# Output projection of the mixing stage as three fp32r products, with new places and load times for its rows

## The chip, the cores and the metric

One core of a Trainium2 chip. The metric is the device time of one execution of the whole layer, in microseconds (us), median of several runs. The core has five engines that run their own instruction streams and wait for each other on semaphores: TensorE (matrix products and transposes, in the profile PE, its weight loads PEld), VectorE (DVE), ScalarE (ACT), GpSimd (POOL) and SyncE (SP), which issues nearly all transfers. PSUM has eight banks of 512 float32 columns, called ps[:, 0] to ps[:, 7].

## What is computed

A hybrid layer on 1024 tokens of width 1024, with 16 meta tokens ahead:

```python
h = concat(meta, x)
u = rmsnorm(h, norm_mix)
z = u @ w_in
y_a = rwkv7_mix(z[..., :P_A], ...)       # 8 heads of 64, a recurrence over the tokens
y_b = retention_mix(z[..., P_A:], ...)   # 4 heads of 128, a recurrence over chunks
mixed = concat(y_a, y_b)
h = h + mixed @ w_out                    # (1024 x 1024) @ (1024 x 1024): the changed product
u = rmsnorm(h, norm_ffn)
h = h + hier_moe(u, ...)                 # top-1 group, top-2 of 32 experts, gated MLP
out = rmsnorm(h, norm_final)[:, 16:]
```

All inputs and outputs are float32.

## The kernel before

Three stages follow each other with a barrier of all engines between them. There are no planners: the order on each engine is the order in which its function issues its instructions.

**project** (lines 224 to 1226). u = rmsnorm(h) is made in nine tiles t: 16 meta rows, then eight tiles of 128 rows. For a tile, SP loads x into h_in[t % 3] (load_x, L323, which waits for u_ready), ScalarE squares and sums it (square, L454), VectorE adds epsilon and later multiplies by the root and the gain (norm, L721), GpSimd takes the power -0.5 (L699), TensorE turns it into PSUM (turn, L1064), ScalarE copies the high part u_hi (high, L463) and VectorE subtracts it for the low part u_lo (low_rows, L732). w_in comes in 30 blocks of 128 columns, split in w_hi (ScalarE, split, L471) and w_lo (VectorE, low, L739). A unit (n, r) (unit, L1073) is block n times one of three ranges of tokens, in 24 products (w_hi u_hi, w_hi u_lo, w_lo u_hi for 8 slices) of 344 or 352 columns. The order of the first units and turns is written out at L1191 to L1213. One load brings all the constants (L350), the identity that the transposes need among them, and TensorE begins by waiting for it.

**mix** (lines 1254 to 2261). Eight tiles t = 1 to 8 of 128 tokens, each with the recurrences of both head groups. On every engine a function body(t) holds one tile's work; inside it stands the closing work of the tile before, n = t - 1: normalising y and the gate, the output projection, the residual, the second rmsnorm and the routing. TensorE's body(t) is, in order: cross products (g_ab, g_ak, g_rk), ret_rows_0(n), chunks for l2, l2_t and q_m, l4, l4_t, l3_t, turn_y(n), chunks l8 and inv4, rwkv_rows_0(n), ret_rows_1(n), chunk inv8, rwkv_rows_1(n), turn_ret(t), the chunks x_t, x_m, z0, x2_t, ret_scores(t+1), x3_t, ret_keys(t+1), turn_h2(n), w, ranks and route(n), ret_inner(t+1), to_features (m_t, rz, n_m), ret_cross(t+1), the states and y. "Chunks" are 16 products of 64x64x64. ret_rows and rwkv_rows are the four calls of project(n, c, ...) at L1999 to L2005: each multiplies four transposed 128x128 blocks of mixed rows (mixed_b from the retention, mixed_a from the rwkv part) with 512 columns of w_out, in float32:

```python
mm = pe.matmul(ps[:, 6 + c, :], rows[:, k_, :], w_out[:, at_, c * 512:(c + 1) * 512], ...)
```

The mixed rows come to SBUF by one ScalarE copy each from the bank where they were turned (mixed_rows_a, mixed_rows_b, L1458 to L1462). On VectorE the chain inv_1, inv_2, inv_3, inv_4, inv_ready (L1772 to L1801) builds a triangular inverse step by step from what TensorE's chunks give, with keep, b_centre, choose_group, residual(n, 0), b_gate, choose_first, choose_second and residual(n, 1) between its steps.

The rows of a tile are 24 feature rows (a, b, k, r, q, kr, four each; fm) and 9 token rows (v, a, bh, kh, kd, rv, rg, gate, bonus; tm). Both have two places, by t % 2, and SP loads them a tile ahead: load_fm and load_tm (L1345 to L1353), in the loop at L1398. w_out is one load of 4 MB (L1377). 15 blocks of zeros are stored to y_slots from h_t at the start (L1386). At the end SP loads the first expert's gate and up matrices in four pieces each (first_weights, L1391), the one after y0_done(7), the other after inv_ready(8). They go to the place of tm1 and what stands behind it.

**dispatch_and_experts** (from L2264). Gathers each expert's rows, and makes three fp32r products with high and low parts (product, L2807) for every expert. It begins when the routing's last result, slot_row, and the stores of u2 are there.

## Time and profile before

| | us |
|---|---|
| three timed runs | 1551.6, 1559.14, 1559.41 (median 1559.14) |
| the profiled execution | 1555.97, its span 1554.1 |
| TensorE busy, share of the span | 92% |
| VectorE, ScalarE, GpSimd busy | 1023.9, 698.9, 563.2 |
| mean granted TensorE clock | 0.957 |
| stages in the span | project to 459, mix 464 to 919, experts from 921 |

All times below are of the profiled execution, in us from the span's start. A row of the timeline has the start, the time from the first start to the last end of what is merged in the row, the engine, the line and the operation with what it writes and reads, and in brackets the idle time of the engine ahead of it and what ended that. TensorE's products overlap by their fill, so the distance between two starts is the price of one in a stream, not its own duration.

### The profile page before, as it was taken

To read this page: it belongs to the slowest core of one execution; us is meant where nothing else is said; L and a number is where in the kernel's file an instruction comes from. 1 tells how busy PE (TensorE), PEld (TensorE's weight loads), DVE (VectorE), ACT (ScalarE), POOL (GpSimd) and SP (SyncE) were. 2 spreads that over 40 slices of the span, in tenths; PEclk is the share of its full clock that TensorE was granted. 3 is DMA by queue.
4 is the path that set the end of the run, shared out by engine and by line. 5 is a ranking of instruction groups with operands and counts; after the bars stand their busy time and mean duration, and the time that the engine had idled before them with its cause. 6 is when DMAs were issued, how large, how long until landed. Compare 5 with 4: busy or idle time off the path is not lost. (4 is left out here: it accounts for less than half of the span.)

```text
span 1554.1 us, 32619 instructions
## 1 busy us (share of the span) xinstructions
PE 1426.6 (92%) x14222; PEld 1225.4 (79%) x14222; DVE 1023.9 (66%) x1174; ACT 698.9 (45%) x678; POOL 563.2 (36%) x198
## 2 busy tenths in 40 slices
PE   5999999999989899998999858999999999999990
PEld 4899999999988777687778637788888888888870
DVE  5456555444213656666577536999989899777757
ACT  4434442212212112121222126777777777777752
POOL 1001101000000000000000027777787878999975
PEclk9999999999997999999999869999999999999995
DMA  5124354543429732333232329999999999999968
GB/s 206 42 96 140 120 157 131 158 127 111 130 63 343 253 106 96 105 130 132 69 115 72 111 90 423 413 405 408 411 412 402 407 400 406 416 413 420 413 249 326
DMA packets 113575, 366.24 MB, mean 236 GB/s; under 512 B 10896, under 2 KB 70672, under 8 KB 100384
## 3 DMA queue, kind: packets, MB, share of 16 engines
q1 hardware_dynamic: 100640, 318.33, 54.2%
q0 software_dynamic: 6912, 25.17, 4.6%
q10 hardware_dynamic: 5904, 20.97, 3.3%
q8 instruction: 96, 1.57, 0.4%
q14 instruction: 23, 0.19, 0.0%
HBM read 295.47 MB, written 68.98 MB: 235 GB/s over the span
## 5 line engine op out<-in xcount | busy, mean ns | idle before, releaser
L1085 PE MATMUL ps<-u_hi,w_hi 128*128 128x352 f32 (+1 forms) x720 | 239.4, 332 | 6.9 <-DVE u_lo L736 6.8
L1085 PE MATMUL ps<-u_lo,w_hi 128*128 128x352 f32 (+1 forms) x720 | 235.0, 326 | 0.0
L1085 PE MATMUL ps<-u_hi,w_lo 128*128 128x352 f32 (+1 forms) x720 | 234.0, 325 | 0.0
L2426 POOL TENSOR_TENSOR down_lo<-down_raw,down_hi 128x1024 fp32r<-128x1024 f32 x31 | 151.2, 4878 | 62.2 <-ACT down_hi L2495 62.2
L2426 POOL TENSOR_TENSOR gate_lo<-gate_raw,gate_hi 128x1024 fp32r<-128x1024 f32 x32 | 161.4, 5045 | 22.1 <-ACT gate_hi L2495 22.1
L2593 DVE TENSOR_TENSOR down_lo<-down_raw,down_hi 128x3072 fp32r<-128x3072 f32 x31 | 125.5, 4049 | 41.8 <-ACT down_hi L2495 41.8
L1085 PEld LDWEIGHTS ps<-u_hi,w_hi 128*128 128x128 f32 x720 | 138.6, 193 | 13.9 <-issue 10.6
L2593 DVE TENSOR_TENSOR gate_lo<-gate_raw,gate_hi 128x3072 fp32r<-128x3072 f32 x32 | 130.8, 4086 | 13.7 <-ACT gate_hi L2495 13.4
L1085 PEld LDWEIGHTS ps<-u_lo,w_hi 128*128 128x128 f32 x720 | 138.6, 192 | 0.0
L1085 PEld LDWEIGHTS ps<-u_hi,w_lo 128*128 128x128 f32 x720 | 138.5, 192 | 0.0
L2593 DVE TENSOR_TENSOR up_lo<-up_raw,up_hi 128x3072 fp32r<-128x3072 f32 x32 | 126.0, 3937 | 15.1 <-ACT up_hi L2495 14.7
L1438 POOL TENSOR_TENSOR mix_stat<-mix_stat,minus_half 128x4 f32<-128x4 f32 x8 | 8.2, 1024 | 344.6 <-DVE mix_stat L1715 344.6
L2495 ACT ACTIVATE gate_hi<-gate_raw 128x4096 fp32r<-128x4096 f32 x32 | 116.4, 3638 | 17.1 <-SPq L2354 13.9
L2495 ACT ACTIVATE down_hi<-down_raw 128x4096 fp32r<-128x4096 f32 x31 | 112.7, 3636 | 19.6 <-ACT y_out L2516 19.6
L2426 POOL TENSOR_TENSOR up_lo<-up_raw,up_hi 128x1024 fp32r<-128x1024 f32 x32 | 116.6, 3644 | 4.0 <-ACT up_hi L2495 3.5
L2495 ACT ACTIVATE up_hi<-up_raw 128x4096 fp32r<-128x4096 f32 x32 | 116.1, 3627 | 0.3 <-DMA up_raw<-in_moe_w_up 0.3
L2811 PE MATMUL ps<-gate_hi,x_hi 128*128 128x512 f32 x256 | 102.2, 399 | 6.9 <-POOL gate_lo L2426 6.7
L2811 PE MATMUL ps<-up_hi,x_hi 128*128 128x512 f32 x256 | 102.9, 402 | 3.3 <-DVE up_lo L2593 2.3
L2811 PE MATMUL ps<-gate_lo,x_hi 128*128 128x512 f32 x256 | 100.8, 394 | 0.0
L2811 PE MATMUL ps<-gate_hi,x_lo 128*128 128x512 f32 x256 | 100.8, 394 | 0.0
L2811 PE MATMUL ps<-up_hi,x_lo 128*128 128x512 f32 x256 | 100.2, 391 | 0.0
L2811 PE MATMUL ps<-up_lo,x_hi 128*128 128x512 f32 x256 | 99.7, 390 | 0.0
(397 smaller groups left out, 3041.7 us busy)
## 6 DMA issues: line engine op xcount, KB each, us to landing
down_raw<-in_moe_w_down SPq DMA_DIRECT2D x32, 2048.0 KB, 11.0
gate_raw<-in_moe_w_gate SPq DMA_DIRECT2D x31, 2048.0 KB, 10.5
up_raw<-in_moe_w_up SPq DMA_DIRECT2D x31, 2048.0 KB, 9.6
tm_rows<-tm_stage SPq DMA_DIRECT2D x32, 512.0 KB, 3.3
y_slots<-y_out ACTq DMA_DIRECT2D x31, 512.0 KB, 11.6
w_raw<-in_w_in SPq DMA_DIRECT2D x30, 512.0 KB, 3.7
tm<-tm_rows SPq DMA_DIRECT2D x8, 1792.0 KB, 9.2
y_slots<-h_t SPq DMA_DIRECT2D x15, 512.0 KB, 7.8
```

Of the source, the lines that this page charges most:

```text
L1085: mm = pe.matmul(z_of(n, r_), w[n % 3][:, k_, :], a[:, k_, c0:c1], start=(k_ == 0 and i == 0), stop=(k_ == KD - 1 and i == 2))
L1438: pool.tensor_tensor(stat[:, 5, 0:HB], stat[:, 4, 0:HB], half[:, 0:HB], ALU.pow).then_inc(sem("rstd_b"), 1)
L2426: pool.tensor_tensor(lo[e % 2][:, cut:, :], raw[e % 2][:, cut:, :], hi[:, cut:, :].bitcast(F32), ALU.subtract).then_inc(sem(f"{name}_lo2_r ...
L2495: act.activation(hi[:], raw[b][:], ACT.Copy).then_inc(sem(f"{name}_hi_ready"), 1)
L2593: dve.tensor_tensor(lo[b][:, :cut, :], raw[b][:, :cut, :], hi[:, :cut, :].bitcast(F32), ALU.subtract).then_inc(sem(f"{name}_lo_ready"), 1)
L2811: mm = pe.matmul(ps[:, bank, :], a[:, k, :], w[:, k, cols], start=(k == 0 and i == 0), stop=(k == ks - 1 and i == 2))
```

## The change

In the projection of the mixing stage w_out is kept in a high part w_hi and a low part w_lo (both fp32r), and so are the mixed rows (a_hi, a_lo, b_hi, b_lo). Each float32 product becomes three fp32r products. ScalarE makes the high parts, VectorE the low parts of the rows and four of w_out's eight slices, GpSimd the other four:

```diff
+                def project(c, hi, lo, at_, first, last):
+                    cols = slice(c * 512, (c + 1) * 512)
+                    for k_ in range(4):
+                        for i, (rows, w) in enumerate(((hi, w_hi), (lo, w_hi), (hi, w_lo))):
+                            mm = pe.matmul(ps[:, 6 + c, :], rows[:, k_, :], w[:, at_ + k_, cols],
+                                           start=(first and k_ == 0 and i == 0), stop=(last and k_ == 3 and i == 2))
...
                 def rwkv_rows_0(n):
-                    pe.wait_ge(sem("mixed_a_t"), n)
-                    project(n, 0, mixed_a, range(4), False, True).then_inc(sem("proj0_done"), 1)
+                    if n == 1:
+                        pe.wait_ge(sem("w_out_lo_ready_a"), 4)
+                    pe.wait_ge(sem("a_hi_ready"), n)
+                    pe.wait_ge(sem("a_lo_ready"), n)
+                    project(0, a_hi, a_lo, 0, False, True).then_inc(sem("proj0_done"), 1)
```

VectorE (in body(t); low_a also behind a_gate in the tail, where choose_first follows it):

```diff
+                def low_a(n):
+                    dve.wait_ge(sem("a_hi_ready"), n)
+                    tt(a_lo[:].rearrange("p k t -> p (k t)"), ps[:, 7, :], a_hi[:].rearrange("p k t -> p (k t)").bitcast(F32), ALU.subtract, "a_lo_ready")
...
                     tt(inv[:], inv[:], ps[:, 4, :], ALU.add, "inv_3")
+                    if n:
+                        low_a(n)
                     keep(t, 0)
...
                     dve.tensor_copy(x_m[:], ps[:, 4, :]).then_inc(sem("x_m_ready"), 1)
                     if n:
+                        low_b(t, 5)
                         h_variance(n)
                         norm(n)
...
                     tt(x_p[:], x_p[:], ps[:, 5, :], ALU.add, "x_p_ready")
+                    if t == 1:
+                        low_b(1, 7)
...
                        bank_pair(2), ALU.add, "rz_t_ready")
+                    if t == 1:
+                        for k in range(4, 8):
+                            w_low(k)
                     state_first(t)
```

ScalarE's w_high(k) (1024 elements each) stand in body(1): k = 0, 1 ahead of mixed_rows_b(1), 2, 3 behind it, 4 to 7 behind m_t. GpSimd has w_lo of k = 0 to 3 behind rstd_b(1).

The rows get one place each, except v and r, which have two by the parity of t. Each load waits for the last use of the tile before:

```diff
+                def load_next(t):
+                    sp.wait_ge(sem("g_rk_done"), t - 1)
+                    if t >= 3:
+                        sp.wait_ge(sem("rz_t_ready"), t - 2)
+                        sp.wait_ge(sem("y0_done"), t - 2)
+                    load_fm(t, "a", "k")
+                    load_fm(t, "r", "r")
+                    load_tm(t, "v", "v")
...
+                for t in range(1, NT):
                     n = t - 1
+                    if n:
+                        if t + 1 < NT:
+                            load_next(t + 1)
+                        sp.wait_ge(sem("mixed_a_ready"), n)
                         load_tm(t, "gate", "bonus")
                     if t + 1 < NT:
+                        sp.wait_ge(sem("mixed_b_ready"), t)
+                        load_tm(t + 1, "rg", "rg")
+                        sp.wait_ge(sem("z0_a_done"), t)
+                        load_tm(t + 1, "a", "a")
+                    if n:
+                        store_h2(n)
+                        load_h(t)
+                        store_u2(n)
+                    if t + 2 < NT:
+                        load_retention(t + 2)
+                    sp.wait_ge(sem("n_m_done"), t)
+                    if t + 1 < NT:
+                        load_tm(t + 1, "bh", "kh")
+                    if t + 2 < NT:
+                        load_heads(t + 2)
+                    for i in range(2 * n, min(2 * t, EXTRA)):
+                        sp.dma_start(y_dram[(NE + i) * P:(NE + i + 1) * P, :].rearrange("p (a c) -> p a c", c=2 * P),
+                                     zero[:].unsqueeze(1).to_broadcast([P, D // (2 * P), 2 * P])).then_inc(sem("zero_stored"), 16)
+                sp.wait_ge(sem("mixed_b_ready"), NTX)
+                first_weights(0, "moe_w_gate")
+                first_weights(1, "moe_w_up")
                 store_h2(NTX)
                 store_u2(NTX)
```

load_retention(t) loads kd behind kv_done(t-1) and rv behind inner_done(t-1), load_heads(t) loads q and kr behind cross_done(t-1). The blocks of zeros are written two per tile from a row of 256 zeros. Several temporaries share a place: q_m that of ak_t, x_m that of ld_t, x_t that of ld, x2_t that of l4_t, x_p that of lo, rz_t that of l2, w_m that of z0. The meta rows' semaphores of tile 1 are merged into three counters.

In **project**, every x tile has a place of its own (in rows that are used later) and its statistics a column of their own, u has four places, load_x waits for nothing, and the epsilon is added by ScalarE behind the square:

```diff
                 def load_x(t):
-                    if t >= 3:
-                        sp.wait_ge(sem("u_ready"), t - 2)
-                    sp.dma_start(h_in[t % 3], x[(t - 1) * P:t * P, :]).then_inc(sem(f"h_loaded{t % 3}"), 16)
+                    sp.dma_start(h_in[t], x[(t - 1) * P:t * P, :]).then_inc(sem(f"h_loaded{t}"), 16)
...
-                sp.dma_start(consts[:], d["consts"]).then_inc(sem("consts_loaded"), 16)
+                sp.dma_start(ident, d["consts"][:, 0:P]).then_inc(sem("ident_loaded"), 16)
+                load_x(2)
                 load_w(0)
-                load_x(2)
+                load_x(3)
                 load_w(1)
...
+                load_w(2)
+                sp.dma_start(consts[:, P:], d["consts"][:, P:]).then_inc(sem("consts_loaded"), 16)
...
+                    act.wait_ge(sem("mean_square"), t + 1)
+                    act.activation(stat[0:w, 1, t:t + 1], stat[0:w, 0, t:t + 1], ACT.Copy, bias=1e-6).then_inc(sem("mean_eps"), 1)
```

On ScalarE the order becomes square 0, 1, 2, high 0, square 3, high 1, split 0, high 2, square 4, high 3, split 1. On VectorE: norm 1, low_rows 0, norm 2, norm 3, low_rows 1, low_rows 2, low 0, low_rows 3, low 1. On TensorE weights(1) moves from ahead of unit(0, 0) to ahead of unit(1, 0), and the wait for the other constants stands ahead of block 2.

## Rows read from the trace of the kernel before

**Rows 1.** The page's first part: busy us, share of the span, instructions.
```profile
PE 1426.6 (92%) x14222; PEld 1225.4 (79%) x14222; DVE 1023.9 (66%) x1174; ACT 698.9 (45%) x678; POOL 563.2 (36%) x198
```

**Rows 2.** Windows: length, busy us (x) of PE, PEld, DVE, ACT, POOL, clock, DMA.
```profile
467.00:479.00 12.00, 10.86 (x242) 10.27 (x236) 4.80 (x14) 2.03 (x6) 0.00 (x0) 0.50 1.00 332
...
527.00:576.00 49.00, 47.54 (x1056) 37.49 (x1054) 28.16 (x49) 11.08 (x19) 3.20 (x3) 1.00 0.36 115
...
1000.00:1450.00 450.00, 447.54 (x2113) 369.50 (x2112) 405.00 (x214) 346.16 (x176) 377.18 (x101) 1.00 1.00 409
```

**Rows 3.** The line L1438, once per mixing tile: ns min/median/max, first and last start.
```profile
L1438 POOL TENSOR_TENSOR mix_stat<-mix_stat,minus_half x8: 1007/1007/1143, 506.4 to 850.1; 128x4 f32<-128x4 f32 x8
```

**Rows 4.** Timeline, two weight loads in the projection: start, us, engine, line, operation.
```profile
788.30 0.19 PEld L2003 LDWEIGHTS ps<-w_out,mixed_b 128*128 128x128 f32 x1 [0.24 <-issue]
...
788.73 0.19 PEld L2003 LDWEIGHTS ps<-w_out,mixed_b 128*128 128x128 f32 x1 [0.24 <-issue]
```

**Rows 5.** Timeline of TensorE, expert stage: the first and last of 22 products.
```profile
1199.77 0.39 PE L2811 MATMUL ps<-down_hi,hid_lo 128*128 128x512 f32 x1
...
1204.54 0.39 PE L2811 MATMUL ps<-down_hi,hid_lo 128*128 128x512 f32 x1
```

**Rows 6.** Timeline, the middle of a steady tile.
```profile
748.94 0.60 ACT L1456 ACTIVATE mixed_a<-ps 128x512 f32<-128x512 f32 x1 [0.92 <-PE ps L1885]
...
749.03 0.42 DVE L1535 TENSOR_TENSOR kept<-state,decay 128x256 f32<-128x256 f32 x1
...
750.84 3.70 PE L2003 MATMUL ps<-w_out,mixed_a 128*128 128x512 f32 x8
...
753.63 0.19 DVE L1644 TENSOR_TENSOR t_log<-logits,t_pick 128x32 f32<-128x32 f32 x1
...
755.28 0.68 DVE L1535 TENSOR_TENSOR inv<-inv,ps 128x512 f32<-128x512 f32 x1
...
757.91 1.15 PE L1895 MATMUL ps<-inv,l 64*64 64x64 f32 x32
```

**Rows 7.** Timeline, the tail of the mixing stage.
```profile
889.86 0.60 ACT L1456 ACTIVATE mixed_a<-ps 128x512 f32<-128x512 f32 x1 [9.93 <-PE ps L1885]
...
904.17 0.69 DVE L1535 TENSOR_TENSOR h<-h_res,ps 128x512 f32<-128x512 f32 x1 [3.40 <-PE ps L2003]
...
918.77 0.18 DVE L1876 CAST slot_row<-slot_sum 128x32 int32<-128x32 f32 x1
```

**Rows 8.** Timeline, the start of the kernel.
```profile
11.05 1.06 ACT L460 ACTIVATE tm_stage<-tm_stage 128x1024 f32<-128x1024 f32 x1 [1.17 <-DMA tm_stage<-in_x]
...
24.40 0.63 PE L1085 MATMUL ps<-u_hi,w_hi 128*128 128x352 f32 x1 [3.70 <-DVE u_lo L736]
...
40.78 0.62 PE L1085 MATMUL ps<-u_hi,w_hi 128*128 128x344 f32 x1 [3.11 <-DVE u_lo L736]
```

**Rows 9.** Timeline of VectorE, the first mixing tile.
```profile
513.60 0.69 DVE L1535 TENSOR_TENSOR memory<-scratch,ps 128x512 f32<-128x512 f32 x1
...
515.84 1.22 DVE L1535 TENSOR_TENSOR w_m<-z,ps 128x1024 f32<-128x1024 f32 x1 [1.55 <-PE ps L1895]
...
525.09 0.42 DVE L1535 TENSOR_TENSOR state<-kept,ps 128x256 f32<-128x256 f32 x1 [5.98 <-PE ps L1929]
```

**Rows 10.** The page's costliest groups: count, busy us, mean ns of one, idle before.
```profile
L2593 DVE TENSOR_TENSOR down_lo<-down_raw,down_hi 128x3072 fp32r<-128x3072 f32 x31 | 125.5, 4049 | 41.8 <-ACT down_hi L2495 41.8
...
L2426 POOL TENSOR_TENSOR up_lo<-up_raw,up_hi 128x1024 fp32r<-128x1024 f32 x32 | 116.6, 3644 | 4.0 <-ACT up_hi L2495 3.5
```

**Rows 11.** Transfers issued from 459 to 530: count, size, median us to landing.
```profile
fm<-fm_rows SPq DMA_DIRECT2D x2, 512.0 KB, 8.6
```

**Rows 12.** Timeline, SP's last loads of the stage and TensorE's last n_m product.
```profile
865.92 13.98 SPq L1395 DMA_DIRECT2D up_raw<-in_moe_w_up x4
...
875.96 0.45 PE L1920 MATMUL ps<-tm 64*64 64x64 f32 x8
```

**Rows 13.** Timeline of TensorE, a gap inside a steady tile.
```profile
737.00 0.47 PE L1907 MATMUL ps<-fm 64*64 64x64 f32 x2 [3.99 <-issue]
```

More of the change, by code:

```diff
@@ L234, in project @@
         tm = tile(s, "tm_stage", [P, 6, SEQ])
-        h_in, u, gain = [tm[:, b, :] for b in range(3)], [tm[:, 3 + b, :] for b in range(2)], tm[:, 5, :]
+        u, gain = [tm[:, 1 + b, :] for b in range(4)], tm[:, 5, :]
         by_tile = lambda i: tm[:, i, :].rearrange("p (t c) -> p t c", c=P)
@@ L1195, in _ @@
                 weights(0)
-                weights(1)
                 pe.wait_ge(sem("u_hi_ready"), 4)
@@ L1201, in _ @@
                 turn(5)
+                weights(1)
                 unit(1, 0)
@@ L1278, in mix @@
+        v_even, gate_bonus, r_even = sb("v_even", DA), sb("gate_bonus", 2, DA), sb("r_even", 4, P)
+        zero = sb("zero", 2 * P)
+        w_hi = tile(s, "w_out_hi", [P, KD, D], F32R)
+        w_lo, w_raw = env["two_names"](s, "w_out_lo", [P, KD, D], F32R, "w_out_raw", [P, KD, D])
+        assert nc.sbuf_base <= first_at
+        router_w = sb("router_w", KD, NR)
         gain, router_b, ffn_gain = sb("norm_ffn_rows", D), sb("router_b", NR), sb("ffn_gain", KD)
         h_in, h2, u2, h2_t = sb("h_res", D), sb("h2", D), sb("u2", D), sb("h2_t", KD, P)
-        mixed_a, mixed_b = sb("mixed_a", 4, P), [sb(f"mixed_b{b}", 4, P) for b in range(2)]
@@ L1281, in mix @@
-        ld_t, ld, lo, ak_t, rb_t, rk_t, l2, l4_t, inv, x_m, x_t, x2_t, x_p, q_m, rz_t, y = (
-            sb(n, DA) for n in ("ld_t", "ld", "lo", "ak_t", "rb_t", "rk_t", "l2", "l4_t", "inv",
-                                "x_m", "x_t", "x2_t", "x_p", "q_m", "rz_t", "y"))
-        l8, scratch = l2, sb("scratch", DA)
+        a_hi, a_lo, b_hi, b_lo = (sb(n, 4, P, dt=F32R) for n in ("a_hi", "a_lo", "b_hi", "b_lo"))
+        ld_t, ld, lo, rb_t, rk_t, l2, inv, y = (sb(n, DA) for n in ("ld_t", "ld", "lo", "rb_t", "rk_t", "l2", "inv", "y"))
@@ L1286, in mix @@
+        l8, rz_t, q_m, x_m, x_t, x2_t, x_p, scratch = l2, l2, ak_t, ld_t, ld, l4_t, lo, sb("scratch", DA)
         y_sq = ret_sq = crossed = memory_d = scratch
-        z0, w_m, m_t = sb("z0", 2, DA), sb("w_m", 2, DA), sb("m_t", 2, DA // 2)
+        z0, m_t = sb("z0", 2, DA), sb("m_t", 2, DA // 2)
+        w_m = z0
         state, kept = [sb(f"state{i}", DA // 2) for i in range(2)], [sb(f"kept{i}", DA // 2) for i in range(2)]
@@ L1444, in _ @@
                 rstd_b(1)
+                for k in range(4):
+                    pool.wait_ge(sem("w_out_hi_ready"), k + 1)
+                    pool.tensor_tensor(w_lo[:, k, :], w_raw[:, k, :], w_hi[:, k, :].bitcast(F32), ALU.subtract).then_inc(sem("w_out_lo_ready_a"), 1)
                 for t in range(2, NT):
@@ L1458, in mixed_rows_a, with w_high @@
                 def mixed_rows_a(n):
-                    copy(mixed_a[:].rearrange("p k t -> p (k t)"), ps[:, 7, :], "y_turned", n, "mixed_a_t")
+                    copy(a_hi[:].rearrange("p k t -> p (k t)"), ps[:, 7, :], "y_turned", n, "a_hi_ready")
                 def mixed_rows_b(t, bank):
-                    copy(mixed_b[t % 2][:].rearrange("p k t -> p (k t)"), ps[:, bank, :], "y_ret_turned", t, "mixed_b_t")
+                    copy(b_hi[:].rearrange("p k t -> p (k t)"), ps[:, bank, :], "y_ret_turned", t, "b_hi_ready")
+                def w_high(k):
+                    copy(w_hi[:, k, :], w_raw[:, k, :], f"w_out_loaded{k // 4}", 16, "w_out_hi_ready")
                 def mean_square(n):
@@ L1516, in body @@
                     else:
+                        for k in range(0, 2):
+                            w_high(k)
                         mixed_rows_b(1, 7)
+                        for k in range(2, 4):
+                            w_high(k)
                     if t + 1 < NT:
@@ L1838, in body @@
                        bank_pair(2), ALU.add, "rz_t_ready")
+                    if t == 1:
+                        for k in range(4, 8):
+                            w_low(k)
                     state_first(t)
@@ L1858, in _ @@
                 a_gate(NTX)
+                low_a(NTX)
                 choose_first(NTX - 1)
@@ L1996, in m_state @@
                         mm = pe.matmul(out_, m_toks("kh")[:, f], m_toks("v")[:, f], start=False, stop=True)
[L1997 to L2004 removed]
+                    mm.then_inc(sem("m_products_done"), 1)
+                def project(c, hi, lo, at_, first, last):
[4 more added lines that the diff above has]
+                                           start=(first and k_ == 0 and i == 0), stop=(last and k_ == 3 and i == 2))
                     return mm
```

286 lines of the change are left out of this document (144 added, 142 removed).

## The prediction, made before the changed kernel was run

> **What bounds the kernel now.** I read four views, in this order. The page's busy shares come first: TensorE is busy for 92% of the span [rows 1]. An average over three stages says little, so the windows come next. In the steady part of the mixing stage TensorE is busy for 47.5 of 49 us at full clock, VectorE for 28, ScalarE for 11, and the DMA share is 0.36; in the expert stage TensorE is busy for 447.5 of 450 us and the DMA engines are full [rows 2]. One operation that runs once per tile starts at 506.4 and, seven tiles on, at 850.1: a tile takes 49.1 us [rows 3]. So what TensorE does in a mixing tile is what the tile costs, as long as no other engine's chain becomes the later one, and the expert stage is touched by the change only through the moment at which it starts. Third, the timeline of one tile gives the price of the projection and what VectorE does beside it. Fourth, the timelines of the first 45 us and of the tail show the two ends, where TensorE waits.
>
> **The projection, the main term.** It is 16 float32 products of 512 columns per tile, in four calls of four. A call shows as eight records [rows 6], and its weight loads start 0.43 us apart [rows 4], so a product takes 2 x 0.427 = 0.853 us and a call 3.41 us. The tile pays 16 x 0.853 = 13.65 us. The change makes 48 fp32r products of the same 512 columns. The expert stage has exactly this form, a 128x128 fp32r weight changed for every product: from 1199.77 to 1204.54 there are 21 intervals, 0.227 us each [rows 5]. So 48 x 0.227 = 10.90 us, a saving of 2.75 us per tile. The projection of tile n runs in the body of tile n+1, so seven times (n = 1 to 7) in the part that TensorE bounds: 7 x 2.75 = **-19.3 us**.
>
> **What is late next inside a tile.** Each call is 0.69 us shorter. ret_rows_0 opens the tile, with nothing on VectorE late there. The middle pair is the tight place. The two operations added to VectorE, low_a and low_b, are 512-wide subtractions from PSUM, priced by inv, the same kind: 0.68 us [rows 6]. low_a waits for a_hi, which ScalarE finishes at 748.94 + 0.60 = 749.54; before, VectorE went on with kept at 749.03 [rows 6]. So low_a runs from about 749.65 to 750.35, and what stands behind it on VectorE (keep, b_centre, choose_group, the first residual, inv_4) moves by about 1.25 us. rwkv_rows_0 began at 750.84 [rows 6], so it need not wait for a_lo. choose_group's last operation ran from 753.63 [rows 6]; now it ends at about 755.05. The residual and inv_4, which before waited for the projection's first half, now wait for this chain (the half is done at 750.84 + 12 x 0.227 = 753.6), and inv_4 runs from 755.7 to 756.4, where it ran at 755.28. TensorE comes to the chunks that need it at 750.84 + 24 x 0.227 + 0.1 = 756.4, where it came at 757.91 [rows 6]. The two arrive together: I take 0.1 us of wait per tile, 0 to 0.6 as bounds, **+0.7 us** for seven. low_b stands behind x_m and pushes h2's norm by 0.7 us beside four chunks of TensorE's; I take nothing, at most 0.3 per tile.
>
> **The tail.** Tile 8's projection has nothing to hide under it but its first call, which runs while VectorE normalises y. a_hi ends at 889.86 + 0.60 [rows 7], low_a adds 0.8 us, and each of the three calls left is at least 0.69 us shorter until the residual at 904.17 [rows 7]: 0.8 - 2.1 = **-1.3 us**, bounds 0 and -2.1. choose_first and choose_second slide behind low_a, under the first of these calls. The routing behind is unchanged.
>
> **The start.** TensorE begins the first block at 24.40 us [rows 8], after four x tiles have been squared, scaled, turned and split. x2's square starts at 11.05 [rows 8], when its transfer has landed behind the constants (1090 columns, 545 KB by the code) and w block 0, and x3 is issued only after a u_ready. In the change 64 KB of identity stands there instead, every x tile has its own place, and x3 is the seventh transfer: the bytes ahead of it and its own are what they were for x2, so it lands at about 11.1. From then on ScalarE is the chain: square 3 with its accumulator read and the new add of epsilon 1.5, u_hi 1, w_hi 0 and u_hi 2 at about 1.05 each (all 1024 wide, as the square of [rows 8]), square 4 again 1.5, about 0.5 for the turn behind it, u_hi 3 1.05. That ends at 18.8; VectorE's u_lo 3 adds 1.22 (the price of 1024 elements, w_m in [rows 9]): 20.1. low(1) is covered by unit(0,0), since weights(1) is moved behind that. So -4.3 us. The next wait, 3.11 us before unit(0,1) at 40.78 for u_lo 6 [rows 8], goes by the same steps to about 36.3. **-4.3 us**, bounds -2 (ScalarE's chain has more gaps than I see) and -6. From there TensorE bounds the stage. The other constants and w block 2 are issued last, some 20 us ahead of their use: nothing.
>
> **The first mixing tile.** On VectorE low_b(1) comes between x_p and memory_decay(2). memory_next started at 513.60 and w_m at 515.84 [rows 9]. low_b waits for b_hi, which ScalarE has at 514.3, and pushes memory_next to 515.8 and w_m to 516.5: +0.65 us. Four w_low of 1.22 us, 4.9 in all, come before state_first, where VectorE sat idle for 5.98 us before 525.09 [rows 9]; but they are fed by four w_high on ScalarE behind m_t and end only at about 524.7, and TensorE had lost 2.5 us in a gap there, which may not come again: bounds 0 and +2.5, taken +1. GpSimd gets four w_lo of 1024 elements at 3.64 us [rows 10], from about 511.5 to 526, before the first power that it owes, near 534. Against these costs stand the 15 zero stores of 0.5 MB, behind which the DMA queues were full until 514, and which now go out two per tile. TensorE's gaps in this tile make some 5 us; how many of them go is not shown: 0 to -5, taken -1.2. Sum **+0.5 us**, bounds -4 and +4.
>
> The Trainium skill's GPSIMD Engine Reference (Specifications) says that GpSimd contends with VectorE operations that have two SBUF inputs. In the expert stage, where both run, VectorE's 3072 elements take 4.05 us [rows 10], against 3 x 1.22 = 3.66 alone, so 11% more. By that rule VectorE's 11 us of work under GpSimd's four would take 1.2 us more, and the sum would be that much higher; no row of the mixing stage has the two together.
>
> **The loads with one home.** Each is issued behind its last use and needed one tile later. The tightest in the steady part is q and kr, issued behind cross_done and needed some 36 us later, for a landing time of 8.6 us for 512 KB even between full queues [rows 11]. In tile 1 that pair is only some 7 us apart, with queues that are empty by then: 0, at most 2 us. On SP's queue every load stands behind n_m_done and cross_done of its tile, which come before the next g_rk_done; nothing is late. The end has one tight place: both first expert matrices now wait for n_m_done(8), which is at 875.96 + 0.4 [rows 12]. Four pieces are issued in 13.98 us [rows 12] with a landing after each, so eight take about 34 us, h2's and u2's stores 4 more: 38 us. The routing leaves 918.77 [rows 7] - 876.4 = 42.4 us, about 41 after. Hidden by 3 us; with slower pieces it costs up to 2.
>
> **Sum.** -19.3 + 0.7 - 1.3 - 4.3 + 0.5 = -23.7 us against the profiled execution's 1555.97 us (its span is 1554.1): 1532.3 us. The timed runs lie between 1551.6 and 1559.41, their median 3 us over the profiled one. I predict **1532 us**.
>
> **Rivals.** (A) VectorE bounds the tile. For it: after the middle pair it has no room left, and two more operations. Against: it is busy for 28 of 49 us [rows 2]. Then what the middle pair saves is given back, 7 x 1.38 = 9.7 us: 1542 us. (B) The mixing stage's beginning gains more. From 467 to 527 the first tile takes 60 us for what is 49 us elsewhere, and begins at a clock of 0.50 with full DMA queues [rows 2]. If the gaps go and the clock rises sooner, 7 us more: 1525 us. (C) Slower: TensorE runs out of instructions inside the tiles. One steady tile has a gap of 3.99 us at 737.00, put down to nothing that the profile shows [rows 13]. The projection brings 32 more products, each with its weight load, and SP issues more and smaller transfers. One such gap in each of seven tiles, 28 us, eats the gain (1560 us, no change); from eight gaps on the kernel is slower by over 0.5%, and with two per tile it takes 1588 us. Against: the seven tiles show one of this size, and none inside the projection. (D) The change does not do what it says, because the fp32r products don't keep the expert stage's pace: at the low clock's double price, 0.453, they take 21.8 us per tile, +57 us in all. Against: the steady tiles' clock is 1.00 [rows 2] and TensorE gets busier, not idler.
>
> The Trainium skill's page Runtime: NRT & Kernel Launch (Instruction fetch mechanics) says that the fetch is streamed and mostly hidden, by which (C) costs nothing; the row of 3.99 us is not hidden, if it is a fetch.
>
> **How the numbers follow.** My forecast (1527 to 1538) has a chance of 0.68, (A) 0.13, (B) 0.12, (C) 0.03 (a third of it slower, the rest no change), (D) 0.01, and 0.03 stand for small losses that add up to no change. About 0.5%, 7.8 us, is what a measurement of this kernel can tell from no change. Faster by more 0.93, within 0.05, slower 0.02. The range goes from 1522, with (B) and the start's bound, to 1543, with (A) and the scatter of the runs.
>
> **What would show it.** Right: products 0.227 us apart; a tile of about 46.4 us; less than 0.6 us of wait before the chunks that need inv_4; the first product of block 0 near 20 us; slot_row's copy some 23 us earlier; no wait of TensorE for a load. Wrong: a tile above 47.5 us (look at inv_4 behind low_a), TensorE waiting for a DMA, or a barrier into the expert stage that waits for u2's store.

## The result, and the profile of the changed kernel

The changed kernel takes **1545.1 us** (median of 20 runs), the kernel before, beside it, 1556.3 us (20 runs). The ratio is 0.9926, with a 95% interval of 0.991 to 0.9943. So it is faster by 0.74%, and what I forecast as -24 us is -11 us. The direction was right, the time lies outside my range.

The changed kernel's profiled execution takes 1548.4 us, 3.3 over the median, and its span is 1546.6, so 7.5 less than the span before; the parts below add up to these 7.5 and not to 11. Where that comes from is read from the starts of one operation, GpSimd's power for the variance of y, once per tile: first and last start in the kernel before, and then in the changed one.

```profile
L1434 POOL TENSOR_TENSOR mix_stat<-mix_stat,minus_half x8: 1637/1644/1645, 534.1 to 884.8; 128x8 f32<-128x8 f32 x8
```
```profile
L1483 POOL TENSOR_TENSOR mix_stat<-mix_stat,minus_half x8: 1635/1644/1645, 526.1 to 875.5; 128x8 f32<-128x8 f32 x8
```

The first one comes 8.0 us earlier. From there seven tiles take 349.4 us, where they took 350.7: **1.3 us less, where my sum had 18.6**. (After_again, the changed kernel profiled once more, has 352.7 there, so a single execution tells this to some 3 us.) The tail gives nothing and the experts take some 2 us more, within what they differ by between the profiled executions (634.6 to 638.4 us). The tiles are nearly the whole miss. The start did what I said, as the timeline of the changed kernel shows beside [rows 8]:

```profile
20.13 0.63 PE L1091 MATMUL ps<-u_hi,w_hi 128*128 128x352 f32 x1 [2.46 <-DVE u_lo L741]
...
35.19 0.63 PE L1091 MATMUL ps<-u_hi,w_hi 128*128 128x344 f32 x1 [2.46 <-DVE u_lo L741]
```

The projection, too, runs nearly at the pace that I took. The timeline of TensorE in a steady tile (the answer to [rows 5] and [rows 6]):

```profile
779.41 0.39 PE L2086 MATMUL ps<-w_out_hi,b_lo 128*128 128x512 f32 x1
779.64 0.40 PE L2086 MATMUL ps<-w_out_lo,b_hi 128*128 128x512 f32 x1
...
780.81 0.39 PE L2086 MATMUL ps<-w_out_hi,b_lo 128*128 128x512 f32 x1
```

Six intervals in 1.40 us are 0.233 each, not 0.227. Forty-eight of them take 11.2 us.

Then what does TensorE wait for? The view of TensorE's waits, over the seven tiles: line, releaser, us in total, times, longest. First the kernel before, then the changed one. L1907 and L1989 are the cross products, L1895 and L1977 the chunks.

```profile
PE ps L1907 <- issue: 7.4, 6, 4.0
PE ps L1895 <- issue: 1.9, 3, 1.0
PE ps L1907 <- DVE y L1535: 1.1, 3, 0.4
```
```profile
PE ps L1989 <- issue: 20.1, 9, 4.2
PE ps L1989 <- DVE y L1595: 1.1, 3, 0.4
PE ps L1977 <- ACT l_t L1508: 0.7, 1, 0.7
PE ps L1977 <- issue: 0.7, 2, 0.4
```

The waits for engines are what they were. "Issue", waiting for nothing that the profile shows, went from 9.3 to **20.8 us**. The longest such gap in the timeline, with the last row of products ahead of it:

```profile
617.34 0.68 PE L1989 MATMUL ps<-fm 64*64 64x64 f32 x28 [0.37 <-DVE y L1595]
622.19 0.37 PE L1989 MATMUL ps<-fm 64*64 64x64 f32 x2 [4.17 <-issue]
```

The DMA view of three stretches around this gap points to the cause: 613.2 to 619.9, 619.9 to 621.1, and 621.1 to 622.2.

```profile
DMA packets 1932, 1.74 MB, mean 259 GB/s; under 512 B 46, under 2 KB 1825, under 8 KB 1932
q1 hardware_dynamic: 1932, 1.74, 86.7%
y_slots<-zero SPq DMA_DIRECT2D x2, 512.0 KB, 8.2
fm<-fm_rows SPq DMA_DIRECT2D x1, 512.0 KB, 6.9
```
```profile
q1 hardware_dynamic: 208, 0.20, 48.0%
q8 instruction: 1, 0.02, 5.0%
```
```profile
q1 hardware_dynamic: 58, 0.06, 15.8%
```

For 6.7 us there is no instruction packet, only data: the two zero blocks and q to kr, which the change issues behind cross_done and n_m_done. Then one 16 KB packet of instructions runs (queue q8), and about 1.2 us after its end TensorE goes on. In the seven tiles there are 58 such packets for 7365 products, as many weight loads and some 140 semaphore instructions: 256 TensorE instructions to a packet. In the cross products 128 records with their loads, so one packet's worth, run in 2.09 us, and here they fill exactly the time between two gaps:

```profile
569.39 2.09 PE L1989 MATMUL ps<-fm 64*64 64x64 f32 x128 [1.78 <-issue]
573.15 0.33 PE L1989 MATMUL ps<-fm 64*64 64x64 f32 x5 [1.67 <-issue]
```

Two such packets never start less than 3.2 us apart in these tiles. The tile's densest stretch uses instructions up faster than they come, and its reserve is small.

This holds for more than one gap. The seven tiles of the two kernels have 20 gaps put down to issue, and every one of them ends 1.1 to 1.5 us after an instruction packet has landed. How late that packet is can be counted: 256 TensorE instructions back from the first product behind a gap is the moment at which TensorE began the block before (call it the entry). Ahead of the gap of 4.17 us the packet starts 4.75 us after the entry, with 1.26 MB of data in between. The seven tiles of all 18 profiled executions have 172 such gaps over 0.4 us. In 27 of them hardly any data moved in the first microsecond after the entry (under 0.02 MB), and the packet came 0.4 to 1.6 us after it, by the median 1.1; in the 145 others the median is 3.1 us, the longest 5.7. (The count is off a little where records are missing.)

So there are two parts. With nothing else in the queues TensorE can begin a block some 1.1 us (delay) + 1.0 (packet) + 1.4 (until TensorE goes on, the median) = 3.5 us after the entry, an estimate from these rows, and a stretch that uses its block up in 2.09 us must wait. The rest is the data's. If of each gap I put down to the data what the delay has over 1.1 us, it is 15 of 20.8 us in the changed kernel and 5 of 9.3 in the kernel before, again an estimate.

The Trainium skill's page Runtime: NRT & Kernel Launch (Instruction fetch mechanics) says that the instruction memory is refilled in 16 KiB blocks of 256 instructions over the engine's own DMA queue. The trace agrees (58 packets, 0.95 MB). It also says that this is hidden because instructions are issued more slowly than they are filled in. Here the measurement decides: it is not hidden, for 20.8 us of 349.

Behind a long gap comes a second cost. Windows of 2 us around the gap; the third number from the end is the granted clock:

```profile
618.00:620.00 2.00, 0.02 (x1) 0.00 (x0) 2.00 (x5) 0.00 (x0) 0.00 (x0) 1.00 1.10 379
620.00:622.00 2.00, 0.00 (x0) 0.00 (x0) 1.93 (x4) 0.00 (x0) 0.00 (x0) 0.96 0.31 106
622.00:624.00 2.00, 1.81 (x67) 1.81 (x67) 0.48 (x2) 0.00 (x0) 1.64 (x1) 0.50 0.07 21
624.00:626.00 2.00, 2.00 (x16) 1.58 (x9) 2.00 (x4) 0.00 (x0) 0.00 (x0) 0.69 0.21 47
626.00:628.00 2.00, 2.00 (x16) 1.40 (x16) 1.93 (x4) 0.00 (x0) 0.00 (x0) 1.00 1.06 307
```

TensorE stood still for 4.17 us, and the clock falls to 0.50, the 1.2 GHz level, for about 3 us: over the end of the cross products and the first of the projection. Over the seven tiles the mean clock tells what this adds up to (the window of the kernel before, then of the changed one):

```profile
534.00:885.00 351.00, 338.39 (x7248) 266.57 (x7246) 222.92 (x485) 76.99 (x132) 22.68 (x22) 0.98 0.33 108
```
```profile
526.00:875.00 349.00, 325.13 (x7365) 292.42 (x7364) 231.25 (x497) 76.94 (x132) 22.45 (x21) 0.97 0.40 122
```

I count (1 - clock) times the length as the time lost to the low clock, an estimate whose last digit is worth 3.5 us: 7.0 before, 10.5 after (6.8 and 11.9 with the trace's clock to four digits, 0.9805 and 0.9658). Take both losses away and a tile takes (350.7 - 9.3 - 7.0) / 7 = 47.8 us before and (349.4 - 20.8 - 10.5) / 7 = 45.4 after: 2.4 us less, and 16 x 0.853 - 48 x 0.233 = 2.5 (13.65 - 11.2). As far as this rounding lets me see, the gain of the projection is all there; gaps and clock took some 15 us of it back.

### The profile page after: what moved, and what is told of

It is laid out like the page before. It is cut to its first block and busy times, and to the rows that moved or that the text cites. A ratio compares the mean times of both kernels' runs of the same rounds, so it can differ in the third digit from the quotient of the medians.

```text
span 1546.6 us, 32982 instructions
## 1 busy us (share of the span) xinstructions
PE 1409.7 (91%) x14350; PEld 1252.4 (81%) x14350; DVE 1037.0 (67%) x1185; ACT 707.9 (46%) x695; POOL 574.0 (37%) x202
## 5 line engine op out<-in xcount | busy, mean ns | idle before, releaser
L2685 DVE TENSOR_TENSOR gate_lo<-gate_raw,gate_hi 128x3072 fp32r<-128x3072 f32 x32 | 130.6, 4082 | 15.3 <-ACT gate_hi L2587 15.0
```

The costliest lines, as they stand in the source:

```text
L2685: dve.tensor_tensor(lo[b][:, :cut, :], raw[b][:, :cut, :], hi[:, :cut, :].bitcast(F32), ALU.subtract).then_inc(sem(f"{name}_lo_ready"), 1)
```

## The experiments

Theory T2 says that data transfers hold up the instruction packets. Theory T1 says that the instructions are too dense whatever the queues hold. They can both hold. The table gives all runs in the same terms: the ratio to the kernel before, the seven tiles (first to last of the power above), the waits for issue and the mean clock in them, and what a tile takes without both losses. Rows with the same chip letter can be held against each other directly; across letters I compare the ratios, with 0.001 worth 1.6 us.

| kernel | chip | median us | ratio, 95% interval | 7 tiles | issue | clock | tile without |
|---|---|---|---|---|---|---|---|
| before | | 1556.3 | 1 | 350.7 | 9.3 | 0.98 | 47.8 |
| changed | | 1545.1 | 0.9926 (0.991, 0.9943) | 349.4 | 20.8 | 0.97 | 45.4 |
| late_all | A | 1537.1 | 0.9866 (0.9824, 0.9909) | 341.6 | 15.3 | 0.97 | 45.2 |
| late_zeros | A | 1538.8 | 0.9878 (0.9846, 0.9909) | 340.1 | 17.4 | 0.98 | 45.1 |
| mix_alone | A | 1551.2 | 0.9969 (0.9944, 0.9993) | 350.8 | 19.9 | 0.95 | 44.8 |
| old_loads | A | 1543.6 | 0.9881 (0.984, 0.9923) | 347.0 | 18.6 | 0.97 | 45.4 |
| spread | B | 1528.7 | 0.9835 (0.9784, 0.9887) | 334.9 | 14.1 | 0.98 | 44.9 |
| zeros_spread | B | 1536.6 | 0.9874 (0.9829, 0.992) | 335.3 | 14.6 | 0.98 | 44.9 |
| phase | B | 1547.7 | 0.9943 (0.992, 0.9966) | 349.6 | 19.1 | 0.96 | 45.2 |
| old_products | B | 1561.1 | 1.0027 (0.9998, 1.0055) | 372.4 | 18.9 | 0.96 | 48.4 |
| after_again | C | 1544.4 | 0.9911 (0.9884, 0.9938) | 352.7 | 20.5 | 0.95 | 44.9 |
| spread_again | C | 1530.8 | 0.9839 (0.9806, 0.9871) | 340.4 | 16.7 | 0.97 | 44.8 |
| spread_half | C | 1532.6 | 0.9842 (0.9816, 0.9869) | 338.7 | 13.5 | 0.97 | 45.0 |
| double_zeros | C | 1552.2 | 0.9977 (0.9958, 0.9995) | 355.8 | 22.2 | 0.94 | 44.6 |
| before_phase | D | 1557.3 | 1.0015 (0.9993, 1.0037) | 354.7 | 14.0 | 0.99 | 48.2 |
| spread_phase | D | 1539.4 | 0.9885 (0.9852, 0.9918) | 344.6 | 19.2 | 0.98 | 45.5 |
| zeros_phase | D | 1539.8 | 0.9889 (0.9857, 0.9921) | 345.3 | 18.3 | 0.98 | 45.7 |
| before_spread | D | 1552.9 | 0.9969 (0.995, 0.9987) | 353.2 | 14.0 | 0.98 | 47.4 |

The last column falls into two groups, 44.6 to 45.7 for the 48 fp32r products and 47.4 to 48.4 for the 16 float32 ones: between kernels that differ in the projection alone or nearly so it is 2.4 to 3.5 us per tile (2.4 to 3.2 with the clock to four digits), in every layout. The rest of what sets the tiles apart is gaps and clock. The profiled execution is one of several, and single ones differ by 5 us or more; part of that lies ahead of the mixing stage, since from unit(0,1) to the last product of w_in the changed kernel takes 415.2 us and late_zeros, with the same code there, 410.9. Compare tiles with tiles, and whole kernels by the ratios.

**late_all and late_zeros.** Both move transfers out of the cross products. In late_zeros, with the zero blocks alone moved:

```diff
                     if n:
+                        sp.wait_ge(sem("g_rk_done"), t)
                         if t + 1 < NT:
                             load_next(t + 1)
+                        zeros(t - 1)
...
-                    for i in range(2 * n, min(2 * t, EXTRA)):
...
```

zeros(t) is the removed loop as a function. In late_all the loads of bh to kh and of q to kr stand ahead of zeros(t - 1), too.

> The changed kernel, but bh to kh, q to kr and the two zero blocks of a tile are issued behind the next tile's g_rk_done, so that no data transfer is issued between n_m_done and the end of the next tile's cross products. Theory T2 (these transfers fill the DMA queues just when TensorE's next 16 KB of instructions must come, and delay them): the gaps put down to issue at the cross products of the steady tiles, 1.8 + 1.7 + 4.2 + 3.4 + 1.2 + 2.0 + 1.7 + 1.5 + 2.6 us and some small ones, about 22 us in all, fall to the 9 or so of the kernel before; the kernel is 10 to 13 us faster than the changed one, near 1534. Theory T1 (the instructions are simply too dense there: 256 of them run in 2.1 us and a fetch takes over 3.4, whatever the queues hold; the shorter projection leaves less time to catch up): no difference beyond 2 us.

> The changed kernel, but only the two zero blocks of a tile (1 MB of 1 KB packets) are issued behind the next tile's g_rk_done. T2: more than half of what late_all gives, 5 to 9 us faster than the changed kernel. T1: no difference beyond 2 us. If late_all gains and this does not, it is bh to kh and q to kr.

Measured: ratios 0.9866 and 0.9878, against 0.9926 and, in after_again, 0.9911 for the changed kernel: 5 to 9 us faster. The two can't be told apart, so what is gained comes with the zero blocks alone. What it does to the instruction packets shows in the DMA view of late_zeros from 610.5 to 617.2, the same part of the same tile (this kernel is there 2.7 us earlier):

```profile
DMA packets 1161, 0.98 MB, mean 146 GB/s; under 512 B 32, under 2 KB 1056, under 8 KB 1159
q1 hardware_dynamic: 1159, 0.95, 44.3%
q8 instruction: 2, 0.03, 1.8%
```

Two instruction packets run, where the changed kernel had none, beside 0.95 MB of data in place of 1.74. So T2 is a cause. But the waits for issue fall only from 20.8 to 15.3 and 17.4 us. Where they lie in late_zeros (L1994 are the cross products, L1982 the chunks):

```profile
PE ps L1994 <- issue: 9.3, 8, 2.1
PE ps L1982 <- issue: 8.1, 7, 1.9
```

In the cross products they fall from 20.1 to 9.3 us, and the chunks, which had 0.7, now have 8.1: the transfers went behind g_rk_done, and six of the seven packets that the chunks wait for have 0.97 to 1.29 MB of data ahead of them. So T2 accounts for much of what is left, too. T1 is what remains where the queues are empty: gaps of up to 1.7 us in both kernels with hardly any data between entry and packet. Both theories hold a part, and neither all.

**mix_alone.** The changed mixing stage behind the first stage of the kernel before (no diff: one function is taken from the other kernel).

> The mixing stage of the changed kernel behind the old first stage (x tiles in three places, constants in one piece). By the shift of the first product of unit (0, 1), 40.78 to 35.19, the start is worth 5 us: this kernel should be 4 to 6 us slower than the changed one, about 6 us faster than the one before. If the start's gain is lost on the way into mixing, it is as fast as the changed one.

Measured: 0.9969, against 0.9926: the start is worth some 6.7 us by these ratios (9 against after_again's 0.9911), more than expected, and more than half of the whole gain is the start's. The profiles don't show it, since this kernel's first stage ran in 410.8 us and the changed one's in 415.2.

**old_loads.** The other half of the question: the old loads with the new products.

```diff
                         sp.wait_ge(sem("y0_done"), n)
                         load_fm(t + 1, "q", "kr")
                         load_tm(t + 1, "v", "rg")
                         load_fm(t + 1, "a", "r")
...
-                        mm = pe.matmul(ps[:, 6 + c, :], rows[:, k_, :], w_out[:, at_, c * 512:(c + 1) * 512],
...
+                        for i, rows in enumerate((hi, lo, hi)):
+                            mm = pe.matmul(ps[:, 6 + c, :], rows[:, k_, :], w_hi[:, at_ + k_, cols],
```

It leaves out w_out's low part, and with it the work of VectorE and GpSimd that makes it.

> The new start and the 48 fp32r products per tile, in the old layout: two homes per row group, all loads of a tile in one batch behind y0_done, zero blocks stored before tile 1. The low part of w_out is left out (its high part stands in its place). T2: the gaps are those of the kernel before, and it reaches what I forecast, 1530 to 1534. T1: the gaps stay near 20 us and it takes 1541 to 1545, like the changed kernel.

Measured: 1543.6 (ratio 0.9881, some 1538 by that, its interval reaching from 1531 to 1544), the issue waits 18.6 us. The waits are T1's number, the time is open between the two. Three gaps of 4.0 to 5.1 us stand in it, where the batch behind y0_done fills the queues. With these loads and the old products it was 9.3 us. So the new loads alone are not to blame: with the shorter projection the old batch collides too.

**old_products.** The loads of the change with the 16 float32 products of before:

```diff
-                        for i, (rows, w) in enumerate(((hi, w_hi), (lo, w_hi), (hi, w_lo))):
-                            mm = pe.matmul(ps[:, 6 + c, :], rows[:, k_, :], w[:, at_ + k_, cols],
...
+                        mm = pe.matmul(ps[:, 6 + c, :], hi[:, k_, :], w_raw[:, at_ + k_, cols],
```

> The changed kernel with the 16 float32 products per tile of the kernel before and none of the high and low parts; start, loads and zero blocks as changed. Against the changed kernel this prices the projection alone: by my 0.853 and the measured 0.234 us it should save 7 x (13.65 - 11.2) = 17 us in the steady tiles; if the gaps eat part of it, the changed kernel is less than 12 us faster than this one. T2: its gaps are about as large as the changed kernel's, near 20 us (the loads are the same), and it takes 1560 or more, slower than the kernel before. T1: the longer projection gives the fetch time, gaps of 10 us or less, about 1550.

Measured: 1.0027, as slow as the kernel before or slower although it has the faster start; issue 18.9 us. That is near T2's number. Loads and zero blocks at n_m_done bring the gaps also without the shorter projection. With old_loads this makes a square: 9.3 us of issue waits with both old, 18.6 and 18.9 with one new, 20.8 with both new. The two parts of the change do not add up; either one is enough. Against this kernel the projection gives 16 us, so under these loads it is worth nearly what the measured intervals give (17).

**double_zeros.** The dose doubled at the same place:

```diff
-for i in range(2 * n, min(2 * t, EXTRA)):
+for i in (i for j in range(2 * n, min(2 * t, EXTRA)) for i in (j, j - NE)):
```

> The changed kernel with four zero blocks of 512 KB behind cross_done of each tile instead of two; the second two go to rows that the experts write later. T2, the transfers hold up the instructions: the two more blocks keep the DMA queues full for some 3 us more, right in the cross products; gaps and low clock grow by 5 to 20 us in the seven tiles, and the kernel is 5 to 20 us slower than the changed one, perhaps slower than the one before. T1 alone: within 2 us of the changed kernel.

Measured: 1552.2, 8 us slower than after_again on the same chip (10 by the ratios). Without zero blocks at this place the ratio is 0.9878, with two 0.9911, with four 0.9977. The waits for issue hardly grow (22.2 against 20.5), the clock in the seven tiles is 0.94 against 0.95, and they take 355.8 us against 352.7. These two profiled executions differ by 2 us only, so they don't show where the whole 8 lie; what they show is more low clock (5 us, with the clock to four digits) than gaps.

**spread, zeros_spread, spread_half.** T1's remedy: the products that need few instructions go between those that need many.

```diff
 cross(0, 256, a_t, b_t).then_inc(sem("g_ab_done"), 1)
+if n:
+    ret_rows_0(n)
 cross(2, 0, k_t, a_t)
 cross(2, 256, b_t, r_t).then_inc(sem("g_ak_done"), 1)
 cross(4, 0, k_t, r_t).then_inc(sem("g_rk_done"), 1)
-if n:
-    ret_rows_0(n)
```

> The changed kernel; the 12 fp32r products of ret_rows_0 are issued between the first 32 cross products of a tile and the other 48, instead of behind all 80, and the work is the same. TensorE takes 2.8 us over the 24 instructions of these products, where 256 instructions of cross products run in 2.09 us. If the gaps come from instructions that are used up faster than they are fetched (T1), they shrink from 22 us in the seven tiles to 8 to 14 and the kernel is 7 to 14 us faster than the changed one; the wait for VectorE's ak_t and rk_t, whose products come 2.8 us later, may take back 0.5 us per tile. If only the zero blocks matter (T2 alone), nothing changes, or it is up to 3 us slower through that wait.

> late_zeros and spread together. late_zeros left gaps of 17 us over 0.5 us each in the seven tiles, nearly all of 1 to 2 us in the cross products. T1 and T2 as two causes that add up: gaps below 8 us, a tile of about 47.2 us, 1528 to 1533. If the gaps only move to another place in the tile: as fast as late_zeros, 1536 to 1540.

> The changed kernel with ret_rows_0 in two halves of six products: one behind the first 32 cross products, one between the next 32 and the last 16. The dense stretches are 32, 32 and 16 products long instead of 32 and 48, and g_ak_done comes 1.4 us earlier than in spread. By T1 the gaps are as small as in spread or smaller: within 3 us of spread, more likely below it. If a dense stretch of 32 is harmless and one of 48 is not, it is 2 to 6 us faster than spread.

Measured: spread 1528.7, in spread_again 1530.8, where the changed kernel has 1544.4 on the same chip. **Some 11 us by the ratios, 14 by the medians, from moving one call**, and the best kernel of this study. In its timeline the last 48 cross products of a tile (96 records) follow the products of ret_rows_0 without a gap:

```profile
564.81 0.80 PE L1989 MATMUL ps<-fm 64*64 64x64 f32 x37 [1.51 <-issue]
...
568.54 1.63 PE L1989 MATMUL ps<-fm 64*64 64x64 f32 x96
569.98 1.10 PE L1977 MATMUL ps<-ld,ld_t 64*64 64x64 f32 x32
```

And its waits over the seven tiles:

```profile
PE ps L1977 <- issue: 7.2, 8, 2.0
PE ps L1989 <- issue: 5.9, 5, 1.5
```

The cross products wait for 5.9 us instead of 20.1, the chunks for 7.2 instead of 0.7: part of the gaps only moved, but no gap is over 2.0 us, and the mean clock is 0.98. (In the profiled execution of spread_again one gap of 3.6 us and one of 2.7 remain.) The wait for ak_t that I feared does not show. With the zero blocks moved as well (zeros_spread) it is not faster, by the median even 8 us slower with overlapping intervals, and its seven tiles take the same: the remedies do not add up. I read that as two ways to break the same coincidence, which no run shows by itself. Halves (spread_half) are as good as the whole.

> The changed kernel as it is, on the chip of the three below, so that they can be held against it. All theories: 0.990 to 0.995 of the kernel before, and gaps and low-clock stretches of some 23 and 12 us in the seven tiles.

> The kernel of spread once more, with more rounds, beside the changed kernel. If the gaps in the dense cross products and the low clock behind them are what ate the gain: 0.982 to 0.986 of the kernel before, 10 to 16 us faster than the changed kernel. If the first run was luck of the order of 0.5%, it lands at 0.988 to 0.992.

**phase, before_phase, spread_phase, zeros_phase.** Half a block of idle instructions ahead of tile 1, so that all later block boundaries fall elsewhere:

```diff
 m_first()
+for _ in range(32):
+    pe.matmul(ps[0:N_META, 0, 0:N_META], ident[0:N_META, 0:N_META], ident[0:N_META, 0:N_META], start=True, stop=True)
```

> The changed kernel with 32 idle products of 16x16 (64 records, 128 TensorE instructions, half of a 16 KB block) before the first cross products of tile 1; they cost 1 to 2 us. Every later block boundary falls half a block later in the code. T1 with blocks: the gaps stand at other places and their sum in the seven tiles changes by 3 us or more, up or down. T2 alone, where only the time of the transfers counts: the same gaps at the same places, shifted by the 1 to 2 us.

> The kernel before, with 32 idle products of 16x16 (128 TensorE instructions, half a block) ahead of tile 1's cross products; by phase against the changed kernel (1547.7 against 1544 to 1545) they cost 1 to 3 us. If the 9 us of gaps of the kernel before are luck of its block boundaries: gaps of 15 us or more in the seven tiles and 8 us or more over the kernel before. If they follow from its loads and products: within 4 us of the kernel before, gaps below 13 us.

> spread with the same half block of idle instructions. If spreading the dense products is a cure: 0.983 to 0.988 of the kernel before, that is at most 4 us over spread. If spread was a lucky alignment: 0.989 to 0.995, like the changed kernel.

> late_zeros with the same half block. If moving the zero blocks out of the cross products is a cure: 0.987 to 0.991 of the kernel before. If it was a lucky alignment: 0.992 to 0.996.

Measured: the changed kernel with it takes 1547.7 (0.9943), some 3 us more. Its gaps stand at other places (3.7 us where 1.67 had been, none over 2.15 in the tile that had 4.17), which speaks for blocks; their sum hardly moves (19.1), by less than the 3 us that I had named. The kernel before stays within the noise, but its issue waits are 14.0 instead of 9.3 us, between my two expectations: a part of its calm is luck. zeros_phase keeps the gain of late_zeros. spread_phase is 7 us above spread, more than the 4 that I had allowed; but phase, which has the same block boundaries and the same idle work, is another 9 us above it (0.9943 against 0.9885). So both remedies are cures in both alignments that were run, worth some 9 us in this one, and spread had a few more in its own. The 9 us hold runs on two chips against each other.

**before_spread.** The same reordering in the kernel before.

> The kernel before, with ret_rows_0 (four float32 products, 3.4 us, 16 TensorE instructions by their records) behind the first 32 cross products instead of behind all 80. The 9 us of gaps and 7 of low clock are all that it can give back, minus a wait for ak_t and rk_t: 0 to 8 us faster than the kernel before. Slower, if that wait decides: the products behind which VectorE's masks stand come 3.4 us later.

Measured: 0.9969, 5 us faster, though its issue waits are 14.0 us in the profiled execution, more than the 9.3 before. I can't say from these rows where the 5 us lie.

## Why the prediction was off, step by step

**The projection (-19.3): right.** 0.233 us an interval instead of 0.227 makes -17.2. The tile without gaps and low clock bears it out, 2.4 us shorter here.

**What is late next inside a tile (+0.7): right.** a_lo runs when I said, and the chunks that need inv_4 wait little, here in the timeline of the changed kernel for the tile that answers to [rows 6]:

```profile
789.20 0.69 DVE L1595 TENSOR_TENSOR a_lo<-ps,a_hi 128x512 fp32r<-128x512 f32 x1 [0.46 <-ACT a_hi L1508]
...
790.51 0.50 PE L2086 MATMUL ps<-w_out_hi,a_hi 128*128 128x512 f32 x1
...
795.25 0.68 DVE L1595 TENSOR_TENSOR inv<-inv,ps 128x512 f32<-128x512 f32 x1
...
796.30 1.15 PE L1977 MATMUL ps<-inv,l 64*64 64x64 f32 x32
```

The weight load of the last line waited 0.37 us for inv; I took 0.1, with 0.6 as bound. Rival (A), VectorE as the bound, is refuted: its time (1542) is near the measured one, but by luck, since TensorE's waits for VectorE are what they were.

**The start (-4.3): right, if small.** The first product of block 0 comes 4.3 us earlier, unit(0,1) 5.6.

**The first mixing tile (+0.5, bounds -4 and +4): within its bounds.** From unit(0,1) to the first power of tile 2's body it is another 2.4 us shorter, which one execution each doesn't resolve: from the first cross product to the first start of the power of [rows 3] it takes 41.2 us in the kernel before and 37.7 in before_spread, whose code is the same up to there. My price for GpSimd was too high: two of its w_lo take 4.7 us, where I had 3.64 each.

**The tail (-1.3): missed.** From the last of the powers to the slot_row copy it takes 33.95 us, as before. low_a costs the 0.8 us that I gave it. But the call that follows runs at the low clock as a whole, as TensorE stands still for 5.49 us ahead of turning y and the clock falls to 0.50. The same call in the kernel before, then the changed one:

```profile
890.51 5.34 PE L2003 MATMUL ps<-w_out,mixed_a 128*128 128x512 f32 x8 [0.69 <-ACT mixed_a L1456]
```
```profile
882.03 0.76 PE L2086 MATMUL ps<-w_out_hi,a_hi 128*128 128x512 f32 x1 [1.50 <-DVE a_lo L1595]
...
883.02 0.63 PE L2086 MATMUL ps<-w_out_lo,a_hi 128*128 128x512 f32 x1
883.45 0.63 PE L2086 MATMUL ps<-w_out_hi,a_hi 128*128 128x512 f32 x1
...
909.45 0.18 DVE L1958 CAST slot_row<-slot_sum 128x32 int32<-128x32 f32 x1
```

There an fp32r product takes 0.43 us, the call 5.3. In the kernel before it took 5.2, at a clock of 0.68, so nothing is saved in that call; the two calls behind it save 0.6 us each, and the routing's products between them, at the low clock, lose 0.4.

**The loads with one home (0): the step that failed.** I asked of each transfer whether it is late for its user, and none is. I did not ask what else uses the queues at that moment. The transfers that the change puts behind n_m_done and cross_done stand in the way of TensorE's instructions, just ahead of the 80 products that use them up fastest. This is rival (C)'s mechanism. I had it, gave it 0.03, and let nothing of it into the sum. Two errors made it small. First, I held against it that the seven tiles show one gap of its size. That gap, [rows 13], is of this kind: its instruction packet landed 1.2 us ahead of 737.00. But the view of waits gives 9.3 us in nine pieces for these tiles, and a mechanism that costs 9 us before the change deserved a term with bounds on both sides, not a rival of all or nothing. Second, I priced it by the gap alone; the clock behind it costs as well. What the runs show in place of my 0: waits for issue of 20.8 us instead of 9.3, and 3.5 to 5 us more lost to the low clock. Of the 18.6 us that I forecast for the seven tiles, 2.0 went to the slower interval, 11.5 to more waiting for instructions, and 3.5, by the rounded clock, to the low clock: 1.6 remain, and 1.3 were measured. That the two agree so closely is the rounding's luck.

That the kernel before was so little disturbed is in part its layout and its longer projection, by the square of old_loads and old_products, and in part the place of its block boundaries, by before_phase (14.0 us of waits instead of 9.3).

## What to carry to other kernels

Where TensorE runs many small products, count its instructions as a flow: how many per microsecond each stretch uses, and what the DMA queues carry when the next 16 KB must come. Keep bulk stores that nobody waits for out of the dense stretches, and put products with few instructions between those with many; here one call moved up gave as much again as the whole change. A gap put down to "issue" is a cost to be forecast, together with the clock that falls behind it.

## What was not expected of the hardware

- TensorE's instructions come as 16 KB packets over a DMA queue of their own, and bulk data delays them: at the gap of 4.17 us the packet came 7.9 us after the one before it, with 1.74 MB of data in the queues; in late_zeros, at the same place of the tile, 4.0 us after it.
- Dense 64x64 products need 256 instructions in 2.09 us; no two packets started less than 3.2 us apart in the seven tiles of the changed kernel.
- After 4.17 us without work the granted clock fell to 0.50 and stayed there until 3 us after TensorE was busy again.
- At the low clock a product of the projection costs 0.43 us instead of 0.233; the call of the tail that ran there took 5.3 us, and its float32 form at a clock of 0.68 5.2.
- The same products run 0.233 us apart in the mixing stage and 0.227 in the expert stage. This was not followed up.
